# Four stages of a two-layer decoder trunk put in another order

## The reference

```
h = rms_norm(x); proj = h @ w_in
x += (sum over 3 branches of sigmoid(gates) * (branch @ w_branch)) @ w_out   # conv, pooling, attention
h = rms_norm(x)
layer 1: x += (silu(h @ w_gate) * (h @ w_up)) @ w_down        # dense, inner width 3584
layer 2: x += sum over top 2 of 8 experts of weight * expert(h)   # inner width 1792 each
h = rms_norm(x); x += sigmoid(h @ ple_w_gate) * (p @ ple_w_proj)
```

## Time and profile before

| | us |
|---|---|
| median of 3 runs | 1253.34 (1252.72 to 1254.72) |
| the profiled execution, its own time | 1253.34 |
| its span, first to last instruction | 1251.6 |
| PE busy in it | 1213.8 (97%) |
| DVE, ACT, POOL busy | 905.8, 727.6, 113.0 |

### The profile page before, as it was taken

The page is one execution under the profiler, slowest core; times in us unless marked ns, Lnnn a source line. Parts: engine busy times, 40 slices in busy tenths (PEclk is TensorE's granted clock), DMA queues, the critical chain, the costliest instruction groups (busy, mean ns, idle before and its releaser), DMA issues.

```text
span 1251.6 us, 15802 instructions
## 1 busy us (share of the span) xinstructions
PE 1213.8 (97%) x5974; PEld 1008.9 (81%) x5974; DVE 905.8 (72%) x882; ACT 727.6 (58%) x694; POOL 113.0 (9%) x131
## 2 busy tenths in 40 slices
PE   8999999999999999999999999999999999999987
PEld 6987787788888877997778778778888888888865
DVE  6777755644554466657765678998888888888985
ACT  5446443644444355335644477777777777777755
POOL 4700000200000010340000100000010000000301
PEclk9999999999999999999999899999999999999998
DMA  9945454756555555554445499999999999999950
GB/s 295 314 149 187 138 190 144 231 175 200 181 188 194 176 188 161 165 191 168 135 169 182 140 321 370 375 370 383 377 390 370 392 372 391 376 391 374 391 209 34
DMA packets 166985, 317.49 MB, mean 254 GB/s; under 512 B 6721, under 2 KB 70465, under 8 KB 166930
## 3 DMA queue, kind: packets, MB, share of 16 engines
q1 hardware_dynamic: 162112, 302.27, 69.2%
q0 software_dynamic: 4112, 13.44, 3.0%
q10 hardware_dynamic: 706, 1.07, 0.3%
HBM read 310.99 MB, written 5.77 MB: 253 GB/s over the span
## 4 chain that ended last, share of the span: by engine, by line
PE 79%; DVE 10%; ACT 6%; issue 4%; DMA 0%; POOL 0%; POOLq 0%; DVEq 0%; ACTq 0%
PE ps L1790 22%; PE ps L1704 10%; PE ps L1532 9%; PE ps L1534 9%; PE ps L1533 9%; PE ps L1777 8%; PE ps L1718 6%; ACT split L627 4%; DVE split L970 4%; PE ps L1548 1%; PE ps L1758 1%; PE ps L1626 1%; DVE M L1343 1%; PE ps L1652 1%; PE ps L1747 1%
## 5 line engine op out<-in xcount | busy, mean ns | idle before, releaser
L970 DVE TENSOR_TENSOR split<-raw,split 128x2048 fp32r<-128x2048 f32 x281 | 644.6, 2298 | 231.0 <-ACT split L627 229.0
L627 ACT ACTIVATE split<-raw 128x2048 fp32r<-128x2048 f32 x281 | 538.2, 1916 | 206.3 <-PE ps L1534 90.0
L1790 PE MATMUL ps<-split,br 128*128 128x512 f32 x1344 | 316.9, 392 | 1.5 <-DVE br L1092 1.0
L1790 PEld LDWEIGHTS ps<-split,br 128*128 128x128 f32 x1344 | 250.0, 188 | 54.8 <-DVE split L970 1.8
L1532 PE MATMUL ps<-split,hT 128*128 128x512 f32 (+1 forms) x416 | 165.2, 397 | 7.9 <-DVE split L970 3.1
L1777 PE MATMUL ps<-split,hT 128*128 128x512 f32 x672 | 160.8, 392 | 2.9 <-DVE hT L1163 2.9
L1534 PE MATMUL ps<-split,hT 128*128 128x512 f32 (+1 forms) x416 | 160.3, 385 | 0.0
L1533 PE MATMUL ps<-split,hT 128*128 128x512 f32 (+1 forms) x416 | 160.1, 385 | 0.0
L1777 PEld LDWEIGHTS ps<-split,hT 128*128 128x128 f32 x672 | 124.8, 188 | 32.1 <-issue 5.8
L1704 PE MATMUL ps<-split,hT 128*128 128x512 f32 x576 | 136.5, 392 | 0.5 <-DVE tmp L1102 0.5
L1704 PEld LDWEIGHTS ps<-split,hT 128*128 128x128 f32 x576 | 107.1, 188 | 23.2 <-DVE tmp L1102 1.2
(11 more groups left out here) (253 smaller groups left out, 1046.3 us busy)
## 6 DMA issues: line engine op xcount, KB each, us to landing
raw<-moe_w_gu_dram SPq DMA_DIRECT2D x96, 1024.0 KB
raw<-moe_w_down_dram SPq DMA_DIRECT2D x56, 1024.0 KB
raw<-w_in_dram SPq DMA_DIRECT2D x45, 1024.0 KB
raw<-ffn_w_gu_dram SPq DMA_DIRECT2D x56, 512.0 KB
raw<-moe_w_gu_dram SPq DMA_DIRECT2D x32, 512.0 KB
raw<-ffn_w_down_dram SPq DMA_DIRECT2D x14, 1024.0 KB
raw<-w_branch_dram SPq DMA_DIRECT2D x12, 1024.0 KB
raw<-w_out_dram SPq DMA_DIRECT2D x8, 1024.0 KB
```

The source lines that it names most:

```text
L627: act.activation(split[:, t % SPLIT, 0, :], raw[:, t % RAW, :], ACT.Copy).then_inc(hi, 1)
L970: dve.tensor_tensor(split[:, t % SPLIT, 1, :], raw[:, t % RAW, :], split[:, t % SPLIT, 0, :].bitcast(F32), ALU.subtract).then_inc(lo, 1)
L1790: ins = pe.matmul(ps[:, 5 if kind == "up" else 4, :], xe[:, sl, 4 * part + k, :], slot(t, sr, 512)[:, k, :], start=part + k + m == 0, stop ...
```

## The change

- **Dense stage**: one pass without a loop over seven blocks of 512 inner columns. Gate tiles (banks 4, 5), up tiles (banks 6, 7) and down tiles are apart, two of each for a block, still 42 tiles and 24 matmuls each; SP fetches the gate and up tiles with one DMA instead of two. The up bank is used again for the block's eight transposes (`turn_dense`), placed behind the first gate tile of the next block. The last two down tiles are taken token block by token block; adds, squares and `norm` of block 0 stand before those of block 1; `Y` of block 0 is turned inside the projection. DVE now does `norm(2, 1)` before `split_lo(u+1)`, and all of `turn_lo(3)` after it.
- **Layer two's first tiles**: `next_turn` three matmuls earlier, `split_hi(u+5)` ahead of `turn_hi(4, (0, 1))`.
- **Routing**: seven constant products behind the logits, eight behind the ranking, none behind the projection; the lists ahead of the whole projection.
- **End**: PE loads its register before expert 7; the jump stands before `scatter` on PE and before the four adds on DVE. DVE mixes adds and `turn_lo(7, ...)`. Half of `turn(7)` moves into the last `quad`, which takes steps of one token block and one half (`QUAD_STEPS`) and ends in another order (`LAST_STEPS`). The stores take the second half first.

```diff
+DENSE_F = D_FF // 512
+DENSE_TILES = tuple(("gate" if j < 2 else "up", 0, j % 2) for j in range(4)) + tuple(
+    (("gate", "up", "down")[j // 2], f - (j > 3), j % 2) for f in range(1, DENSE_F) for j in range(6)) + (
+    ("down", DENSE_F - 1, 0), ("down", DENSE_F - 1, 1))
+DENSE_N = len(DENSE_TILES)
+def gate_tile(f):
+    return 6 * f - 2 if f else 0
+def turn_tile(f):
+    return gate_tile(f + 1) if f < DENSE_F - 1 else DENSE_N - 4
...
+QUAD_STEPS = tuple((i, b, nh) for i, b in QUAD_ORDER for nh in range(2))
+LAST_STEPS = QUAD_STEPS[:-4] + ((2, 1, 0), (3, 1, 0), (2, 1, 1), (3, 1, 1))
...
-        aT_dense = brf[:, 0:2048].rearrange("p (u s k n) -> p u s k n", u=2, s=2, k=2)
+        aT_dense = brf[:, 0:4096].rearrange("p (u s k n) -> p u s k n", u=2, s=2, k=4)
...
-                for nh in range(2):
+                for nh in (1, 0):
...
+            def dense(t0):
+                for j in range(DENSE_N):
+                    for f in range(DENSE_F):
+                        if j == turn_tile(f) + 1:
+                            for b in range(NB):
+                                act.wait_ge(a_turned[0], NB * f + b + 1)
+                                act.activation(aT_dense[:, f % 2, 0, :, tokens(b)],
+                                               ps[:, 6 + b, :].rearrange("p (k n) -> p k n", k=4), ACT.Copy
+                                               ).then_inc(aT_hi[0], 1)
+                    if j == DENSE_N - 1:
+                        for nh in range(2):
+                            mean_square(0, nh, x_ffn, nh + 1)
+                    split_hi(t0 + j + 2)
+                    for f in range(DENSE_F):
+                        if j == gate_tile(f) + 2:
+                            for b in range(NB):
+                                wait_product(act, b, NB - 1, gu_done, f + 1, t0 + gate_tile(f) + 1)
+                                act.activation(sg[:, b, :], ps[:, 4 + b, :], ACT.Silu).then_inc(silu_ready[0], 1)
...
                     if l == 0:
                         if b == 0:
                             split_hi(u + 4)
+                            split_hi(u + 5)
                         turn_hi(4, (2 * b, 2 * b + 1))
-                        if b == 0:
-                            split_hi(u + 5)
...
+            def dense(t0):
+                for j in range(DENSE_N):
+                    for f in range(DENSE_F):
+                        if j == gate_tile(f) + 4:
+                            dve.wait_ge(tile_used, t0 + j)
+                            for b in range(NB):
+                                dve.wait_ge(silu_ready[0], NB * f + b + 1)
+                                dve.tensor_tensor(tmp[:, cols(b)], ps[:, 6 + b, :], sg[:, b, :], ALU.mult
+                                                  ).then_inc(act_ready[0], 1)
+                        if j == turn_tile(f) + 1:
+                            for b in range(NB):
+                                dve.wait_ge(aT_hi[0], NB * f + b + 1)
+                                dve.tensor_tensor(aT_dense[:, f % 2, 1, :, tokens(b)],
+                                                  ps[:, 6 + b, :].rearrange("p (k n) -> p k n", k=4),
+                                                  aT_dense[:, f % 2, 0, :, tokens(b)].bitcast(F32), ALU.subtract
+                                                  ).then_inc(aT_lo[0], 1)
+                    if j == DENSE_N - 1:
                         for b in range(NB):
                             for nh in range(2):
-                                wait_half(dve, b, nh, down_done, 3 * i, t0 + BODY_TILES - 1, i, BODY_TILES)
+                                wait_half(dve, b, nh, down_done, 0, t0 + DENSE_N - 1)
                                 add_half_to_x(b, nh, 2 * b + nh, x_ffn)
+                            if b == 0:
+                                norm(2, 0)
+                    split_lo(t0 + j + 2)
...
+                    add_last(0, 0)
+                    add_last(1, 0)
+                    add_last(0, 1)
+                    turn_lo(7, (0,))
+                    add_last(1, 1)
+                    turn_lo(7, (1,))
+                    split_gate_lo(1)
+                    turn_lo(7, (2, 3))
                     dve.wait_ge(x_moe, 2 * NB)
                 if l == 0:
-                    norm(2, 0)
+                    norm(2, 1)
                     split_lo(u + 1)
-                    norm(2, 1)
-                turn_lo(4 * l + 3, (0, 1))
-                if l:
-                    split_gate_lo(1)
-                turn_lo(4 * l + 3, (2, 3))
+                if l == 0:
+                    turn_lo(3)
...
+            def turn_dense(f):
+                for b in range(NB):
+                    pe.wait_ge(act_ready[0], NB * f + b + 1)
+                    for k in range(4):
+                        ins = pe.transpose(ps[:, 6 + b, k * P:(k + 1) * P],
+                                           tmp[:, b * 512 + k * P:b * 512 + (k + 1) * P], ident[:, :])
+                    ins.then_inc(a_turned[0], 1)
+            def down_part(t, f, part, b):
+                for nh in range(2):
+                    for k in range(2):
+                        lh = [aT_dense[:, f % 2, s, 2 * part + k, tokens(b)] for s in range(2)]
+                        ins = product(ps[:, 2 * b + nh, :], lh, tile_pair(t, D, k, cols(nh)),
+                                      f + part + k == 0, f == DENSE_F - 1 and part + k == 2)
+                    if f == DENSE_F - 1 and part and (b, nh) != (NB - 1, 1):
+                        ins.then_inc(down_done, 1)
+                return ins
+            def dense(t0):
+                first_gate(t0)
+                for j, (kind, f, part) in enumerate(DENSE_TILES):
+                    t = t0 + j
+                    if j < 2:
+                        continue
+                    pe.wait_ge(lo_ready, t + 1)
+                    if kind == "down" and f < DENSE_F - 1:
+                        for b in range(NB):
+                            if part == 0:
+                                pe.wait_ge(aT_lo[0], NB * f + b + 1)
+                            ins = down_part(t, f, part, b)
                         ins.then_inc(tile_used, 1)
+                    elif kind == "down" and part:
+                        for b in range(NB):
+                            for i in range(2):
+                                pe.wait_ge(aT_lo[0], NB * f + b + 1)
+                                ins = down_part(t - 1 + i, f, i, b)
+                                if b == NB - 1:
+                                    ins.then_inc(tile_used, 1)
+                    elif kind != "down":
+                        for b in range(NB):
+                            if part == 0 and kind == "gate":
+                                pe.wait_ge(silu_ready[0], NB * (f - 1) + b + 1)
+                            if part == 0 and kind == "up" and f:
+                                pe.wait_ge(aT_lo[0], NB * (f - 1) + b + 1)
+                            for k in range(4):
+                                ins = product(ps[:, (4 if kind == "gate" else 6) + b, :],
+                                              pair(hT, 4 * part + k, tokens(b)), tile_pair(t, 512, k, slice(0, 512)),
+                                              part + k == 0, part == 1 and k == 3)
+                            if kind == "gate" and part and b == 0:
+                                ins.then_inc(gu_done, 1)
+                        ins.then_inc(tile_used, 1)
+                    for n in range(DENSE_F):
+                        if j == turn_tile(n):
+                            turn_dense(n)
...
+                over = pe.value_load(more_i[0:1, 0:1], min_val=0, max_val=1) if s == 1 else None
                 expert(s, t0, EXPERTS - 1, True)
-                if s == 1:
-                    for nh in range(2):
-                        pe.wait_ge(ye_lo, nh + 1)
-                        for b in range(NB):
-                            scatter(b, nh)
+                return over
...
+                    idle_work(7, 5)
+                if l == 0:
+                    dense(t0 + T_FFN[0])
                 else:
                     pe.wait_ge(sel_ready, 2)
                     pe.matmul(ps[:, 4, 64:72], ones[:, :], sel[:, 0, :], start=True, stop=False)
                     pe.matmul(ps[:, 4, 64:72], ones[:, :], sel[:, 1, :], start=False, stop=True
                               ).then_inc(load_done, 1)
+                    idle_work(8, 5)
+                    lists(1)
                     proj_part(0, 0)
-                    lists(1)
                     proj_part(0, 1)
                     proj_part(1, 0)
                     proj_part(1, 1)
-                    idle_work(8, 5)
                     pe.wait_ge(proj_out, 2 * NB)
-                    experts(1, t0 + T_FFN[1])
-                    more = pe.value_load(more_i[0:1, 0:1], min_val=0, max_val=1)
+                    more = experts(1, t0 + T_FFN[1])
                     with pe.If(more > 0):
```

(18 more changed lines are left out.)

214 lines of the change are left out of this document (43 added, 171 removed).

## The result

The changed kernel takes **1245.99 us** (median of 5 runs, 1245.95 to 1247.76) against 1253.34 for the kernel before (5 runs, 1252.72 to 1254.78): ratio 0.9938, interval 0.9928 to 0.9949. That is 7.35 us less, where the prediction said 4.0. Measured again later with fresh runs of both, the difference is 6.4 us (1247.83 against 1254.23, ratio 0.9957, interval 0.9944 to 0.9969); why the two differ comes with the last experiments. The traced execution of the changed kernel took 1246.11 us, its span is 1244.3, 7.3 less than before.

A forecast was written before the change was run, and what follows sets the result against it. PE, 97% busy, bounds the kernel; only its idle time, low clock and what follows the last matmul can move. Dense -1.1, layer two -1.5, routing +0.3, end -1.7 sum to -4.0: 1253.34 to 1249.3 us, range 1245.8 to 1252.8.

The forecast's parts named there:

- Dense stage: Layer one's dense blocks up to the PLE quad: start wait, turns and end shortened, -1.1 us (0 to -2.3).
- the forecast's own steps: Dense end: adds, rstd, norm, split and turn_lo after last matmul E; quad begins at E+8.4, before E+8.6.
- the term of the start: Start of the dense stage: the second token block's 0.48 us wait behind a DVE split goes, -0.5 us.
- Layer two's first tiles: Layer two's start: second tile begins at 494.8 instead of 496.40, third still waits; -1.5 us (-0.4 to -3.1).
- Routing: Logits to turn of rows: low clock until about 713, projection undiminished behind the lists; +0.3 us (-1.1 to +1.6).
- clock holds: Rival: clock holds in routing and recovers early at the end, -1.4 and -1.4 more, 1246.5 us; chance 0.14.
- The end up to `quad`: Experts' end to last quad: quad at about 1218.4, -1.5 us, less 0.4 for the register's load.
- The step that failed: After the experts: the jump comes first, so scatter begins at 1210.4 + 3.6 = 1214.0 at the latest.
- Inside the `quad`: Last quad: half the transposes move in, 0.9 us, while its low clock gets shorter, -0.5 us.
- The load: Before expert 7: PE's register load, moved there with matmuls queued, costs +0.4 us of a possible 3.6.
- the load dear: Rival: the 3.58 us are the load, open before expert 7 (+3.2), jump cheap; 1251.7 us, chance 0.08.
- Tail: Behind the last matmul: DVE's wait before its second product goes (-0.8), stores start 0.2 us sooner; -1.0 us.

The follow-up runs named there:

- the last experiments: The changed kernel rerun unedited, 1247.83 us; and the changed kernel with turned pieces first, squares late and the routing of the kernel before, 1242.17 us.
- the jump alone: The kernel before, with only PE's load moved before expert 7 and the jump ahead of scatter (on DVE ahead of the adds): 1251.47 us, ratio 0.9979.

## Why the prediction was right and wrong

The direction held, and 1246.0 lies just inside the range (1245.8 to 1252.8); the size was 3.35 us short, by the second measurement 2.4, so about one microsecond of the miss is chance. Point by point, by its own terms:

- **Dense stage, -1.1 forecast, -2.2 measured.** The parts behind the turns came as said: POOL's L500, formerly L512, was blocked (1.51 us, first row below), and PE's wait for `turn_lo` is 0.91 (1.1). From the last matmul to `quad` 0.4 us were gained (0.2 forecast; the forecast's own steps add up to E+8.2, and it took E+8.4), by the turns and the rest of the blocks 0.6 (0.4 forecast), and 0.15 came in earlier. Mis-sized above all is the term of the start: "-0.5 us" for a wait of 0.48. From matmul start to matmul start, 234.25 to 240.91, 25 starts took 6.66 us and not 25 x 0.227 = 5.67, so 1.0 went. The stop with the 0.48 cost 0.75 of it: 0.87 instead of 0.227 from the last matmul ahead of it to the first behind, and 0.34 instead of 0.227 to the next. A smaller stop at 234.55, for which no row shows idle time, cost 0.2 in the same way. The same rows after as in the earlier trace rows:

```profile
459.97 1.51 POOL L500 TENSOR_SCALAR rstd<-ms 128x1 f32<-128x1 f32 x1 [4.50 <-ACT Y L646]
...
463.57 2.28 DVE L956 TENSOR_TENSOR split<-raw,split 128x2048 fp32r<-128x2048 f32 x1
```

- **Layer two's first tiles, -1.5 and -1.75.** Right, with its mechanism: the second tile starts without idle time, the third still waits 1.87, and the clock falls there as before.
- **Routing, +0.3 and +0.2.** Right in its parts: the clock fell at 705.9, behind the narrow products as before, and stayed low half as long; the lists stand 9.5 us behind the first logit product (9.7 before), and PE waits 1.11 us for ACT's emptying ahead of the turn of rows. That this trace shows the kinder case is luck: in two of the nine traces with this routing the clock was low for 6.8 us and the stretch took 18.8 us, near the +1.6 that the forecast named as the bad end. The rival "clock holds" named nearly the measured time (1246.5), but half of its gain was to come from here, and none did; at the end it did hold.
- **The end up to `quad`, -1.1 and -4.5. The step that failed**: "Now the jump comes first: `scatter` begins at 1210.4 + 3.6 = 1214.0 at the latest". The bound is true, but the value was taken at it, and that moves the jump as if it began when PE's array is done. It begins when the sequencer gets there, 3.1 us ahead of the last matmul, and the array has that work in hand: `scatter` began 0.80 us behind that matmul's start, where the forecast has 4.0 (1214.0 less 1210.02). With the gap went the low clock behind it: before, PE worked at half speed from the transposes at 1216.60 to about 1221.8, which is 2.6 us, and the forecast gave back 0.5 in the `quad` and what four transposes instead of 16 save.
- **Inside the `quad`, +0.4 and +2.0.** The wait of 1.41 us for the fourth gate tile was not foreseen. It doesn't come from the `quad`'s earlier start: with jump, or load and jump, behind the scatter the `quad` begins 1.9 and 3.3 us later, measured from the experts' end, and PE waits there as long (1.37 and 1.41); with the jump alone and the old `quad` it begins 4.2 us earlier than before, and PE waits 0.30. It comes with the turns that moved into the `quad`. ACT must copy their results, waits 1.51 us for the last of them, and its copy of the third gate tile, the four squares and the copy of the fourth stand behind that:

```profile
1215.62 0.60 ACT L622 ACTIVATE hT<-ps 128x512 fp32r<-128x512 f32 x1 [1.51 <-PE ps L1539]
...
1230.62 0.50 PE L1524 MATMUL ps<-split,hT 128*128 128x512 f32 x1 [1.37 <-DVE split L962]
...
1228.48 0.50 PE L1530 MATMUL ps<-split,hT 128*128 128x512 f32 x1 [0.30 <-DVE split L976]
```

The first row is of the changed kernel, the second of the one with the jump behind the scatter, the third of the one with the jump alone. ACT's copy of the fourth tile begins 9.0 us behind the `quad`'s start in the changed kernel, 6.7 before and with the jump alone. Nowhere did the prediction ask what its moved turns make late on ACT.
- **The load, +0.4 forecast, 0 measured** (PE is busy across it at 1143). The rival "the load dear" named the wrong one of the two: the load is 0.87 us and the jump 3.3 to 3.8. The Trainium skill, "Advanced Engine Details and Errata", section "Control Flow Timing", which the prediction weighed, gives 108 ns for a compare-and-branch; DVE's 67 ns and the loops' 76 to 211 lie about there, this jump does not. The row that tells them apart was in the trace of the kernel before (L2013, L2014 above). "No row here separates the two" was wrong.
- **Tail, -1.0 and -1.0.** Right; DVE's second product begins 0.03 us behind its sigmoid (1236.64 + 0.69).

## What to carry to other kernels

A gap labelled "issue" can be an instruction of the sequencer, as here: look at the source lines between the two matmuls, their own rows have its length. What it costs depends on how much work the array still has when the sequencer meets it, and that is what stands behind the sequencer's last wait; 3.1 us of such matmuls hid all but 0.2 us of a jump of 3.8. Where a change takes away an idle gap, add the clock that the gap cost and the refilling of the pipe, and ask which engine is late next, of the work that you moved too; and compare two kernels by the marks of their traces, with the clock at each, before believing two microseconds of median.
